# Projecting the queries, keys and values of all heads in one phase ahead of the attention, through DRAM

## The reference, cut

```python
pq, pkv, pkr, hq, hf_f, hf_b, hi, hg, ga, gb = split_cols(h @ lw['w_in'])
q = (rmsnorm(pq, lw['g_q']) @ lw['w_uq']).reshape(B, T, MLA_HEADS, QK_NOPE + QK_ROPE)   # 8 heads, 64 + 32
ckv = rmsnorm(pkv, lw['g_kv'])                                   # 256 wide
kv = (ckv_keys @ lw['w_ukv']).reshape(B, K, MLA_HEADS, QK_NOPE + V_DIM)                 # 64 + 64 a head
s = (einsum(qn, k_nope) + einsum(qr, k_rope)) * scale            # the key's rotary part is the same for all heads
o_mla = softmax(s) @ v
mix = sigmoid(ga) * (o_mla @ w_mla_o) + sigmoid(gb) * (o_hg @ w_hg_o)
x = x + gt1 * (mix @ lw['w_out'])                                # then the ConvGLU and the last norm
```

## Time and profile before

| | us |
| --- | --- |
| median of 3 runs (lowest, highest) | 2327.46 (2326.67, 2330.14) |
| the profiled execution | 2326.68 |
| its span in the trace | 2324.9 |
| attention block: first S step of head 0, of head 7, last V step's end | 853.67, 1175.89, 1204.98 |

### The profile page before, as it was taken

One profiled execution on the slowest core, in us unless ns is written; L12 is line 12 of the kernel. 1 busy time (PEld: TensorE's weight loads), 2 busy tenths in 40 slices (PEclk: granted clock), 3 DMA queues, 4 the chain that ended last, 5 costly groups with the idle time before them and its releaser, 6 DMA issues. The chain is left out here.

```text
span 2324.9 us, 28777 instructions
## 1 busy us (share of the span) xinstructions
PE 2155.3 (93%) x11772; PEld 1962.1 (84%) x11772; DVE 978.6 (42%) x1422; ACT 705.3 (30%) x1028; POOL 789.6 (34%) x529
## 2 busy tenths in 40 slices
PE   7499999999999889999978868999999999999995
PEld 2489999999999867777758857899999999999994
DVE  3604444435133055555524407623443334423438
ACT  1334232323223146566655221221111211111120
POOL 0325261626132115434531641233322322223334
PEclk9699999999999979999999989999999999999997
DMA  6362121112212100000017372221111111011123
GB/s 229 109 208 86 30 59 41 41 41 64 74 41 73 60 5 16 16 31 16 11 70 210 99 145 100 73 64 46 37 46 37 49 43 46 28 55 46 37 72 128
DMA packets 147731, 155.72 MB, mean 67 GB/s; under 512 B 13704, under 2 KB 119761, under 8 KB 147601
## 3 DMA queue, kind: packets, MB, share of 16 engines
q1 hardware_dynamic: 146304, 149.17, 21.4%
q0 software_dynamic: 1296, 4.72, 0.5%
HBM read 127.23 MB, written 26.64 MB: 66 GB/s over the span
## 5 line engine op out<-in xcount | busy, mean ns | idle before, releaser
L129 POOL TENSOR_TENSOR s_w_lo<-s_w_raw,s_w_hi 128x1024 fp32r<-128x1024 f32 x86 | 219.6, 2554 | 525.6 <-ACT s_w_hi L124 525.6
L810 PE MATMUL s_psum<-h_hi,s_w_hi 128*128 128x384 f32 x1008 | 344.3, 344 | 27.6 <-POOL h_lo L250 27.6
L2321 PE MATMUL s_ps<-h_hi,s_w_hi 128*128 128x384 f32 x1056 | 353.1, 334 | 0.7 <-ACT gate_pad L2165 0.7
L2321 PE MATMUL s_ps<-h_hi,s_w_lo 128*128 128x384 f32 x1056 | 352.9, 334 | 0.0
L2321 PE MATMUL s_ps<-h_lo,s_w_hi 128*128 128x384 f32 x1056 | 352.8, 334 | 0.0
L810 PE MATMUL s_psum<-h_hi,s_w_lo 128*128 128x384 f32 x1008 | 337.7, 338 | 0.0
L810 PE MATMUL s_psum<-h_lo,s_w_hi 128*128 128x384 f32 x1008 | 337.3, 337 | 0.0
L810 PEld LDWEIGHTS s_psum<-h_hi,s_w_hi 128*128 128x128 f32 x1008 | 190.6, 190 | 37.5 <-issue 19.4
L2321 PEld LDWEIGHTS s_ps<-h_hi,s_w_hi 128*128 128x128 f32 x1056 | 198.2, 188 | 1.4 <-issue 1.0
L2321 PEld LDWEIGHTS s_ps<-h_lo,s_w_hi 128*128 128x128 f32 x1056 | 198.2, 188 | 0.3
L2321 PEld LDWEIGHTS s_ps<-h_hi,s_w_lo 128*128 128x128 f32 x1056 | 198.2, 188 | 0.0
(11 more groups left out here) (329 smaller groups left out, 3962.8 us busy)
## 6 DMA issues: line engine op xcount, KB each, us to landing
s_w_raw<-in_w_ffn_in SPq DMA_DIRECT2D x44, 512.0 KB, 3.8
s_w_raw<-in_w_in SPq DMA_DIRECT2D x41, 512.0 KB, 4.2
s_w_mod<-in_w_mod SPq DMA_DIRECT2D x8, 2048.0 KB, 8.3
w_raw<-in_w_ffn_out SPq DMA_DIRECT2D x11, 1024.0 KB, 4.9
scratch_gates<-sig SPq DMA_DIRECT2D x48, 192.0 KB, 1.9
merge_gates<-scratch_gates SPq DMA_DIRECT2D x16, 576.0 KB, 3.9
w_mod<-in_w_mod SPq DMA_DIRECT2D x4, 2048.0 KB, 10.3
scratch_o_mla<-o_raw SPq DMA_DIRECT2D x8, 576.0 KB, 3.1
```

The lines of the kernel that those rows point to most:

```text
L129: pool.tensor_tensor(flat[0], flat[1], flat[2], ALU.subtract).then_inc(self.lo_ready, 1)
L810: return pe.matmul(bank(j), wx[c % 2][:, k, :], hx[:, k, j * CH:(j + 1) * CH], start=(k == 0 and n == 0), stop=(k == KD - 1 and n == 2))
L2321: mm = pe.matmul(ps[bank][:, 0:CH], a[s][:, k, :], b[:, k, j * CH:(j + 1) * CH], start=n == 0, stop=n == 3 * KD - 1)
```

## The change

The attention begins with a phase in which all heads are projected, in the order `B_UNITS`: keys by pairs of heads (128 wide, "k"), values token-major for all heads at once (each of ten token tiles against 512 columns, "v"), queries by head in three units of 384 columns ("q"). Six PSUM banks form a ring. The results go to DRAM scratch tensors: keys and values split already, queries as float32 after the rotary part, whose last addition is now POOL's. SP loads head h+2 back at the end of head h (D: k_hi, k_lo and qf; E: v_hi, v_lo, and the store of an output). Per head there stay S, L, V, the maxima M, P, C, one split of the queries (H on ACT, G on POOL), and T, which replaces R: one transpose of the 128x9 maxima, a split into mx_hi (ACT) and mx_lo (DVE), two stores and two loads through DRAM that lay them as row 97 of q_hi and q_lo. The maxima of head 0 are laid between the last units of the phase (FIRST_TOPS). The weight w_ukv is loaded and split in the projection's gate chunks, w_uq at the phase's start. P_lo of tiles 1 to 5 is POOL's, of the others DVE's. The four row stores of the output stage move to slot HG_FIRST + 3 (18) of the projection, and the x loads go ahead of load_wo(2). HeadPrep, PrepBuffers, HeadWeights, PREP_UNITS and PREP_ALONE go. The core of the diff:

```diff
-                    (13, "ckv_out"), (18, "q_square"), (19, "q_sums"), (20, "q_rb"), (21, "q_apply")):
+                    (13, "ckv_out"), (18, "q_square"), (19, "q_sums"), (20, "q_rb"), (21, "q_apply"), (25, "up_load"), (29, "up_split")):
...
+                    if kind == "up_load":
+                        sp.wait_ge(q_split_done, 1)
+                        sp.wait_ge(ckv_out_t, 1)
+                        sp.dma_start(up.raw[:, :, :], io["w_ukv"].rearrange("(k p) n -> p k n", p=P)).then_inc(up_loaded, 16)
...
+                    if s == HG_FIRST + 3:
+                        sp.wait_ge(mod_ready, 1)
+                        for n, (at, g) in enumerate(((2 * KD, 0), (2 * KD, 1), (5 * KD, 0), (5 * KD, 1))):
+                            sp.dma_start(io["rows"][n:n + 1, :].rearrange("a (k p) -> p (a k)", p=P),
+                                         cst.mod[:, at:at + KD, g], allow_slow_non_contiguous=True).then_inc(rows_out, 16)
...
+                    if kind == "up_split":
+                        act.wait_ge(up_loaded, 16)
+                        up.split_hi(act).then_inc(up_hi_ready, 1)
...
+                    if kind == "up_split":
+                        pool.wait_ge(up_hi_ready, 1)
+                        up.split_lo(pool)
...
-PREP_UNITS = (("Q", 0), ("Q", 1), ("Q", 2), ("K", 0), ("K", 1), ("K", 2),
...
+    units = [("k", 0, u) for u in range(3)] + [("v", t, 0) for t in range(10)]
+    for h in range(HEADS):
+        units += [("q", h, u) for u in range(3)]
+        if h % 2 == 0 and h < HEADS - 2:
+            units += [("k", h // 2 + 1, u) for u in range(3)]
+    return units
...
+TOP_UNITS = tuple(("M", u) for u in range(16)) + (("P", 0), ("P", 1), ("C", 0), ("T", 0))
+FIRST_TOPS = {B_UNITS[B_AT["q", 2, 0] + n]: n for n in range(len(TOP_UNITS))}
...
-POOL_LO = (4, 5, 6, 7, 8)
+    ("L", 0), ("S", 2), ("H", 0), ("L", 1), ("M", 0), ("M", 1), ("V", 0), ("M", 2),
+    ("S", 3), ("L", 2), ("M", 3), ("M", 4), ("V", 1), ("M", 5),
+    ("S", 4), ("L", 3), ("M", 6), ("M", 7), ("V", 2), ("M", 8),
+    ("S", 5), ("L", 4), ("M", 9), ("M", 10), ("V", 3), ("M", 11),
+    ("S", 6), ("L", 5), ("M", 12), ("M", 13), ("V", 4), ("M", 14), ("M", 15),
+    ("S", 7), ("L", 6), ("G", 0), ("P", 0), ("P", 1), ("V", 5), ("C", 0),
+    ("S", 8), ("L", 7), ("T", 0), ("V", 6),
+    ("S", 9), ("L", 8), ("V", 7), ("L", 9), ("V", 8), ("D", 0), ("V", 9), ("E", 0),
+    ("S", 10), ("S", 11))
+POOL_LO = (1, 2, 3, 4, 5)
...
+B_RING = 6
...
+        if kind == "T":
+            pe.wait_ge(self.max_step, 2 * h + 2)
+            last = pe.transpose(ps[0:TILES, 0:P], self.maxima[:, :], self.cst.ident[:, :])
...
+            dve.tensor_reduce(self.maxima[:, 0:8], self.tops[:, :, :], axis=AX.X, op=ALU.max).then_inc(self.max_step, 1)
+            dve.tensor_reduce(self.maxima[:, 8:9], ps[:, 0:TC], axis=AX.X, op=ALU.max).then_inc(self.max_step, 1)
...
+            dve.scalar_tensor_tensor(self.mx_lo[0:TILES, :], ps[0:TILES, 0:P], -1.0, self.mx_hi[0:TILES, :],
+                                     ALU.mult, ALU.subtract).then_inc(self.mx_lo_ready, 1)
...
+        act.activation(self.mx_hi[0:TILES, :], self.banks[n % 2][0:TILES, 0:P], ACT.Copy, scale=-1.0).then_inc(self.mx_hi_ready, 1)
...
+        def ring(n):
+            x = n % B_RING
+            return (*ps_s, ps_o)[x // 2][:, x % 2, :]
...
+            for kind, x, u in B_UNITS:
+                unit(kind, x, u)
+                if (kind, x, u) == ("v", 5, 0):
+                    item("F", 0, 0)
+                if (kind, x, u) == ("q", 0, 2):
+                    item("D", 0, 0)
+                    item("E", 0, 0)
+                if (kind, x, u) == ("q", 1, 2):
+                    item("H", 0, 0)
+                    item("G", 0, 0)
+                if (kind, x, u) == ("q", 3, 2):
+                    item("D", 0, 1)
+                if (kind, x, u) in FIRST_TOPS:
+                    item(*TOP_UNITS[FIRST_TOPS[kind, x, u]], 0)
+            item("S", 0, 0)
+            item("S", 1, 0)
+            item("E", 0, 1)
...
+                sp.dma_start(uq_raw[:, :, :], io["w_uq"].rearrange("(k p) n -> p k n", p=P)).then_inc(uq_loaded, 16)
...
+                    if kind == "k" and u == 2:
+                        sp.wait_ge(u_dve, n + 1)
+                        for name, src in (("k_hi", kst_hi), ("k_lo", kst_lo)):
+                            sp.dma_start(io[name][x * P:(x + 1) * P, :], src[:, :].bitcast(F32)).then_inc(k_stored, 16)
+                    if kind == "v":
+                        sp.wait_ge(u_dve, n + 1)
+                        for name, src in (("v_hi", vst_hi[x % 3]), ("v_lo", vst_lo[x % 3])):
+                            dst = io[name].rearrange("(h p) (t n) -> p t h n", p=P, n=VD)[:, x, :, :]
+                            sp.dma_start(dst, src[:, :].rearrange("p (h n) -> p h n", n=VD).bitcast(F32)).then_inc(v_stored[x % 3], 16)
+                    if kind == "q" and u == 2:
+                        sp.wait_ge(u_act, n + 1)
+                        sp.wait_ge(q_roped, 3 * x + 3)
+                        sp.dma_start(io["q"][x * QH:(x + 1) * QH, :], qst[x % 2][0:QH, :]).then_inc(q_stored[x % 2], 16)
...
+                def load_qk(h):
+                    e = h % 2
+                    sp.wait_ge(k_stored, 32 * (h // 2 + 1))
+                    if h >= 2:
+                        sp.wait_ge(s_full, 10 * (h - 1))
+                    for dst, name in ((low.k_hi, "k_hi"), (low.k_lo, "k_lo")):
+                        sp.dma_start(dst[e][0:64, :].bitcast(F32), io[name][h * 64:(h + 1) * 64, :]).then_inc(k_loaded[e], 16)
+                    sp.wait_ge(q_stored[e], 16 * (h // 2 + 1))
+                    if h >= 1:
+                        sp.wait_ge(q_lo_ready, h)
+                    sp.dma_start(qf[0:QH, :], io["q"][h * QH:(h + 1) * QH, :]).then_inc(qf_loaded, 16)
...
+                def load_v(h):
...
+                            sp.wait_ge(q_stored[i], 16 * HEADS // 2)
+                    if h >= 2:
+                        sp.wait_ge(o_full, 2 * (h - 1))
+                    for dst, name in ((v_hi, "v_hi"), (v_lo, "v_lo")):
+                        sp.dma_start(dst[e][:, :, 64:128].bitcast(F32),
+                                     io[name][h * P:(h + 1) * P, :].rearrange("p (t n) -> p t n", n=VD)).then_inc(v_loaded[e], 16)
...
+                    if kind == "T":
+                        rows = [io["mx"][2 * h + i:2 * h + i + 1, :] for i in range(2)]
+                        for ready, row, src in ((top.mx_hi_ready, rows[0], mx_hi), (top.mx_lo_ready, rows[1], mx_lo)):
+                            sp.wait_ge(ready, h + 1)
+                            sp.dma_start(row.rearrange("o (t n) -> (o t) n", n=P), src[0:TILES, :].bitcast(F32)).then_inc(mx_stored, 16)
+                        sp.wait_ge(mx_stored, 32 * (h + 1))
+                        for dst, row in zip((q_hi, q_lo), rows):
+                            sp.dma_start(dst[e][96:97, :].bitcast(F32), row).then_inc(mx_loaded, 16)
...
+                    if n >= B_RING:
+                        pe.wait_ge(u_act, n - B_RING + 1)
+                        pe.wait_ge(u_dve, n - B_RING + 1)
+                    if kind == "k":
+                        cols = slice(x * P, (x + 1) * P)
+                        pairs = [(w[:, k, cols], c[:, k, a:z]) for k in range(2)
+                                 for w, c in ((up.k_hi, low.c_hi), (up.k_hi, low.c_lo), (up.k_lo, low.c_hi))]
+                    if kind == "v":
+                        rows = slice(x * P, (x + 1) * P)
+                        pairs = [(c[:, k, rows], w[:, k, :]) for k in range(2)
+                                 for c, w in ((low.c_hi, up.v_hi), (low.c_lo, up.v_hi), (low.c_hi, up.v_lo))]
+                    if kind == "q":
+                        if (x, u) == (0, 0):
+                            pe.wait_ge(uq_ready, 1)
+                        cols = slice(x * P, (x + 1) * P)
+                        pairs = [(w[:, k, cols], q[:, k, a:z]) for k in range(3)
+                                 for w, q in ((uq_hi, low.qn_hi), (uq_hi, low.qn_lo), (uq_lo, low.qn_hi))]
...
+                        if (kind, u) == ("M", 0):
+                            pe.wait_ge(q_hi_ready, h + 1)
+                            pe.wait_ge(k_loaded[e], 32 * (h // 2 + 1))
...
+                        if u == 0:
+                            pe.wait_ge(q_lo_ready, h + 1)
+                            pe.wait_ge(mx_loaded, 32 * h + 32)
...
+                    if n == 6:
+                        split_uq_hi()
+                    if n == 12:
+                        split_uq_rot()
...
+                    if kind == "v":
+                        if x >= 3:
+                            act.wait_ge(v_stored[x % 3], 32 * (x // 3))
+                        act.activation(vst_hi[x % 3][:, :], ring(n), ACT.Copy).then_inc(u_act, 1)
...
+                    if kind == "H":
+                        act.wait_ge(qf_loaded, 16 * (h + 1))
+                        if h >= 2:
```

(81 more changed lines are left out.)

487 lines of the change are left out of this document (230 added, 257 removed), and 12 rows, old and new, of tables (HEAD_ITEMS, PREP_UNITS).

## The result

The changed kernel takes 2307.66 us (median of 4 runs, 2301.83 to 2307.95) against 2327.43 of the kernel before (4 runs): a ratio of 0.9907, 95% interval 0.989 to 0.9925, 19.8 us faster. The forecast was 2327.9, no change. The measured time lies in the outer range (2298 to 2355) but not in the forecast's own (2316 to 2340), and it moved where the forecast said it would not.

The account below looks back on a forecast made before the run. TensorE, busy 93% of the span, was taken to bound the kernel, by its own work in the heads. 2326.68 - 45.0 (heads) + 59.2 (dense phase) - 13.0 (row stores) = 2327.9 us; own range 2316 to 2340, outer 2298 to 2355.

Parts of the forecast that it names:

- The price of the 256-byte packet: Value stores of the dense phase: 35 ns a packet, bounds 27.5 and 60; a ns is 1.28 us.
- part 2: The dense phase before the heads: S0 of head 0 at 912.9 instead of 853.67, a loss of 59.2 us.
- The mixed row: Earlier profile's 128-byte new_krope store, mixed with a load: 8.4 us of engine time, read as 31 to 48 ns a packet.
- Dear packets: Rival in the dense phase: packets slower than before, 2344.5 us at 48 ns, 2359.9 at 60; chance 0.24.
- DVE as the pace after M0: Dense phase from the first M0: DVE sets the pace, 1.96 us a query unit.
- The wait for the maxima's way: Heads: maxima go through DRAM in 4.3 us, and the next head's S0 waits 1.3 (bounds 0 and 3).
- M0's wait: Heads: M0 stands behind H, an ACT copy behind the exps of S0 to S2; TensorE idles 4.9 us.
- V8's: Heads: V8 waits for the split of step 8, on DVE behind T; 1.0 us idle.
- the work: Heads: TensorE work left in a head after Q, K, X and R leave, 30.8 us.
- the clock: Heads: half clock after the 4.9 us idle costs 1.8 us a head, bounds 0 and 3.5.
- The clock stays up: Rival in the heads: no clock drop in the 4.9 us gaps, 2315.3 us; chance 0.20.
- Part 3: Row stores moved from the output stage into the projection: gain 13.0 us, bounds 9 and 13, hidden in the projection.

Follow-up runs that it names:

- v128: The changed kernel with the values' runs in DRAM halved, 2048 packets of 128 bytes in each value store: 2316.73 us, ratio 0.9958.
- rope: The changed kernel without the second rotary product of the queries on DVE, the sine part left out of the result: 2301.81 us, ratio 0.9893.
- t_late: The changed kernel with H before S2, V0 before M0, and T moved behind S9 and L8: 2284.56 us, ratio 0.9806.
- order: The changed kernel with H before S2 and V0 before M0 and M1: 2276.88 us, ratio 0.9785.

## Why the forecast was wrong, point by point

- **The price of the 256-byte packet** (part 2) is the step that failed. The rows were 27.5 ns for 512 bytes and 31 to 48 for a mix with 128-byte packets, and 76 for 4 bytes; I took it that a smaller packet is dearer and put 35 between them. Measured are 19.0 and, for 128 bytes, 14.2 (v128): from 512 bytes down the price falls. (These two are intervals between packets. By the engines' busy share, as the earlier trace rows were read, they are 17.3 and 13.5, 0.91 and 0.95 of them: the same order.) The mixed row does not fit this price: at 14 ns its 128 new_krope packets are 1.8 us of the 8.4, and the load beside them would have to cost the rest, which no run here shows. 27.5 ns was no lower bound either.
- **What the cheap packets gave.** Sixteen ns at 1.28 us each would be 20.5 us; the first M0 came 14.4 sooner (51.6 after the projection's end for 66.0). Two things hold back the rest. The value stores are issued by 38.3 us after the projection's end, where the forecast had 59.5, so 21.2 sooner, but then they no longer set when the first query store goes out: it goes as POOL's third addition ends (849.66 and 1.01), 3.5 us behind them. And from this store to M0 it is 9.8 us (850.76 to 860.54), where the forecast had 6.5 (862.9 to 869.4), with the loads of qf and the keys at 415 GB/s; ACT waits for qf until 859.32. 21.2 - 3.5 - 3.3 = 14.4.
- **The rule of the Trainium skill** ("DMA: Bandwidth & Descriptors", Specifications), that below 512 bytes an engine reads, modifies and writes, does not show as a price at 256 or 128 bytes here: both are cheaper per packet than 512. "Dear packets", to which it led and which had 0.24, is the rival that the runs exclude. What makes the 4-byte stores of the earlier trace rows cost 76 ns no run here shows; the stretch also moved some 0.5 MB of blocks, about 1.3 us at 415 GB/s, which leaves an estimated 71. The prediction's "it gives no price for 256" holds for that section alone. The same page of the Trainium skill has another section, "Why small descriptors are slow (HBM only)", which I had passed over: a fixed overhead of some 3 cycles for each packet beside beats of 32 bytes. Its form, a fixed part and a part by the byte, is what v128 and the change show. Its size is not: for 256 bytes it makes the overhead 3 of 11 cycles, 27% of the packet's time, and here 19.0 ns stand against 10.9 for an eighth of a 2 KB packet, so 8.1 of 19.0, 43%.
- **DVE as the pace after M0:** wrong engine (rope), and by luck the right number (42.4 for 43.5).
- **The wait for the maxima's way,** 1.3 us a head, was the second step that failed: measured is 0. The way was reckoned right (t_late), but not what covers it: V7, the wait before V8, V8 and V9 stand on TensorE behind mx_hi. It was 9.1 us of the forecast's sum.
- **M0's wait** 4.49 for 4.9, **V8's** 0.87 for 1.0, **the work** 31.6 for 30.8, **the clock** 1.5 for 1.8: right in mechanism and nearly in size. The errors in them cancel: with 0.1 of other waits they make 0.1 us a head more. "The clock stays up" (0.20) is excluded behind 4.5 us and behind 2.2, and is true behind waits of up to 0.9 (order).
- **Part 3** -13.0: right, 12.7 alone, and the projection was not held. Up to the transposes that wait for h_y the changed kernel gains 13.4. The other 1.7 of the output stage's 15.1 lie in the 100 us behind them, where the granted clock was 0.96 in the kernel before, 0.98 in the changed one and 0.97 or 0.98 in the ten others.
- **The projection's 5.6 us** were in no part of the sum, and 5.1 of them are the clock: below. They hide that the change's own parts sum to 43.7 - 53.5 - 15.1 = -24.9.

Sum of the errors: 15.5 too much loss in the dense phase, 8.5 too little gain in the heads, 2.1 in the output stage, less the 5.6 and 0.6 not forecast: 19.9, the distance between the forecast and the profiled run (2307.95).

## What to carry to other kernels

Price small packets by a fixed part and a part by the byte, from two rows of different sizes of the same direction, and do not divide a mixed row by guess. Where two engines are full within a few per cent of each other, say what each would give alone before naming the pace. In the heads here an idle stretch of 2.2 or 4.5 us on TensorE cost some 1.5 us more in clock, waits of up to 0.9 nothing, and waits of 1.3 the one or the other: put the step whose operands are there (V0) in front of the one that waits (M0), and what it waits for (H) ahead of an exp; that was worth 31 us here, more than the whole change, which gave 20.
